# Low parts of the weight tiles made by VectorE instead of GpSimd, in a two-layer diffusion step on one core

## The chip, the core and the metric

The kernel is one program on one core of a Trainium2 chip. TensorE multiplies matrices, VectorE and ScalarE work element by element on SBUF and PSUM, GpSimd on SBUF alone, and SyncE issues most of the DMAs. The engines run apart from each other, each through its own queue in order, and meet at semaphores. In the rows PE is TensorE, PEld its weight loads, DVE VectorE, ACT ScalarE, POOL GpSimd, SP SyncE; a q behind a name (SPq, ACTq) is the engine's queue issuing DMAs. The metric is the device time of one execution in microseconds.

## The reference

Two layers (DEPTH = 2) run over 512 latent tokens and 128 prompt tokens of width 1024. Cut to its core, a layer is:

```python
h = rms_norm(x, g_pre) * (1 + scale) + shift            # scale, shift, gate from silu(cond) @ w_mod
parts = split(h @ w_in)                                 # w_in: 1024 x 10752
y_sg = spatial_gating(sg_u, sg_v, ...)
y_diff = diff_attention(dq, dk, dv, lam)                # 4 heads, two softmax maps per head
y_na = neighbourhood_attention(nq, nk, nv, ...)         # 8 heads, 8 x 16 window and the context keys
y_f = fourier_mix(h)
mixed = sum(sigmoid(merge[b]) * ((y[b] * silu(gate[b])) @ proj[b]) for b in four branches)
x = x + gate * rms_norm(mixed @ w_o, g_post)
```

All of it is in float32. The outputs are the tokens after both layers and the prompt's keys and values.

## The kernel before

TensorE multiplies in the rounded float32 form (fp32r), which keeps fewer bits than float32. So each operand is split into a high part (rounded) and a low part (value minus high part), and a product is three matmuls: high with high, high with low, low with high (`three`, and the loop in the steps F, M and P).

The weights come as 224 tiles ("slots") of 128 x 1024, in the order in which they are used. For slot n: SyncE loads it into `raw`, of which there are two buffers (RAWS = 2), and waits before that for `lo` of slot n-2; ScalarE copies it into `whi`, which rounds it (`high`, five buffers, SPLITS = 5); GpSimd computes `wlo = raw - whi` (`low`). TensorE waits for `lo` of a slot before its first matmul with it.

The order of everything is one list of 1273 steps, `PLAN.seq`. Every engine runs through this list, does its share of each step and waits on semaphores whose counts are worked out from the list. The steps that the prediction speaks of are: HK, HL and TK (the first layer's h, its low part, and the first product with it), VS and VN (sum of squares and norm of sg_v; the power of -1/2 between them is GpSimd's), F (a projection), M and P (a merge gate and a projected branch, each some 7 us of TensorE), S, EX, CB, TP and PV (scores, exponentials, combination of the two softmax maps, transposes, and product with V of one attention unit), NM (normalisation in the neighbourhood attention), DM (one dot product of a deferred modulation tile), FB (back transform of the Fourier branch), T (a wide projection, with the names sgv, dq, dk, dv, wo0 and wo1), Ya, Yb, Xa, Xb and H (from one layer's output to the next layer's h). In the attention stages F, M and P are cut in parts (PART) that fill the gaps between the attention's steps, so that the steps there are short. `FENCE` lets an engine catch up with the others at a change of stage.

`PLAN.issue` says at which step slots are split: slot n at the first step that uses slot n-4, or right after the last use of slot n-5, whichever is later. ScalarE runs `high` at the beginning of that step, GpSimd `low` in its own queue when it comes to the same step.

GpSimd's other work is the powers: one per tile in Xa, VS and Ya, and one for five tiles in NR (`power` and `root`).

Of the kernel before, what the change touches and what calls it, by code (L numbers as in the profile page):

```python
# [167 lines left out]
WIDE = KT  # L168
LEAD = AHEAD
ASIDE = 4  # L170


def parts(steps):
# [216 lines left out]
class Plan:  # L390


    def __init__(self):
# [43 lines left out]
        for n in range(slot):  # L437
            if n < len(lead_in):
                floor = self.at[0, ("HK", lead_in[n])]
            i = max(self.first_of_slot[n - AHEAD] if n >= AHEAD else start,  # L440
                    self.last_of_slot[n - SPLITS] + 1 if n >= SPLITS else start)
            if self.layer[self.first_of_slot[n]] and self.steps[self.first_of_slot[n]] == ("T", "sgv", 3, 0):
                floor = self.at[1, ("T", "sgv", 0, 2)]
            self.issue.setdefault(max(i, floor), []).append(n)
        self.stream, self.entry = [], {}
        waiting = [(sum(first < i for first in self.first_of_slot.values()) + LEAD, ("D", s[1]))
                   for i, s in enumerate(self.steps) if s[0] == "DM"]
# [91 lines left out]
def program(nc, A, O):  # L539
    with ExitStack() as ctx:  # L540
# [184 lines left out]
        def _(pool):  # L725
# [21 lines left out]
            for i, (layer, step) in enumerate(PLAN.seq):  # L747
                count.at(i)
                kind = step[0]
                for s in PLAN.issue.get(i, ()):  # L750
                    low(s)
                if kind == "Xa":
                    j = step[1]
                    pool.wait_ge(sems["epsd"], count.step("epsd"))
                    power(stats[:, XST, 1, j:j + 1], stats[:, XST, 0, j:j + 1])
                elif kind == "VS":
                    j = step[1]
                    pool.wait_ge(sems["xss"], count.step("xss"))
                    root(VST, j, ss[:, 1, j:j + 1], 512)
                elif kind == "Ya":  # L760
                    j = step[1]
                    pool.wait_ge(sems["epsd"], count.step("epsd"))
                    power(stats[:, YST, 1, j:j + 1], stats[:, YST, 0, j:j + 1])
                elif kind == "NR" and step[3] == 1:
                    pool.wait_ge(sems["epsd"], count.step("epsd"))
                    power(rstd[:, 0:TILES], veps[:, 0:TILES])
# [304 lines left out]
        def _(dve):  # L1071
# [20 lines left out]
            if True:  # L1092
# [7 lines left out]
                for i, (layer, step) in enumerate(PLAN.seq):  # L1100
                    count.at(i)
                    b = PLAN.buf.get(i)
                    kind = step[0]
                    hT, act = held(layer)
                    if kind == "FENCE" and i + 1 < len(PLAN.steps):

                        for name, n in count.phase(i):
# [907 lines left out]
```

## Time and profile before

| | us |
|---|---|
| median of 3 runs (1981.74 to 1983.77) | 1981.79 |
| the profiled execution | 1982.85 |
| its span, first to last instruction | 1980.9 |
| TensorE busy in it | 1903.0 |
| VectorE busy | 960.9 |
| ScalarE busy | 678.3 |
| GpSimd busy | 593.8 |

The span is 1.95 us shorter than the execution's own time, which also holds what lies around the instructions. The profiled execution is 1.06 us above the median of the runs. Mean granted clock of TensorE is 0.989 of full speed. Times in the trace are microseconds from the start of the span. "Idle before" an instruction is shown in brackets with what ended it.

### The profile page before, as it was taken

The numbers are of one execution on the slowest core, as the hardware profiler recorded it, in microseconds if no ns is written. First come the engines' busy times: TensorE is split into PE (matmuls) and PEld (weight loads), VectorE is DVE, ScalarE is ACT, GpSimd is POOL, SyncE is SP. The second block draws the span as 40 slices with busy tenths as digits, with TensorE's granted clock in tenths as the row PEclk, the third lists the DMA queues.
The fourth block names the chain that finished last, engine by engine and source line by source line (L and its number), as shares of the span: only waits on it lengthen the run. The fifth ranks groups of instructions, "written<-read, shape, count | busy, mean of one in ns | idle before, by whom it ended". The sixth has DMA issues, their size and how long they took to land.

```text
span 1980.9 us, 31159 instructions
## 1 busy us (share of the span) xinstructions
PE 1903.0 (96%) x12512; PEld 1762.9 (89%) x12512; DVE 960.9 (49%) x1536; ACT 678.3 (34%) x1293; POOL 593.8 (30%) x278
## 2 busy tenths in 40 slices
PE   6799999999999999999999999999999999999997
PEld 3697888989999999999878988988999999999996
DVE  5799788634355462421352144666244546433123
ACT  4322355424433221321352234453334332222221
POOL 2434322222222332233334332222322223323331
PEclk8999999999999999999999999999999999999999
DMA  8444421121111211122332221111212112212231
GB/s 305 145 164 140 164 97 43 54 83 67 65 65 65 94 66 54 65 75 75 128 117 75 91 75 65 49 49 43 96 65 75 54 65 95 75 35 83 75 126 55
DMA packets 50958, 172.16 MB, mean 87 GB/s; under 512 B 6656, under 2 KB 7296, under 8 KB 50816
## 3 DMA queue, kind: packets, MB, share of 16 engines
q1 hardware_dynamic: 41024, 146.60, 21.3%
q10 hardware_dynamic: 9792, 23.58, 3.3%
q8 instruction: 99, 1.62, 0.3%
q14 instruction: 43, 0.35, 0.1%
HBM read 162.82 MB, written 7.34 MB: 86 GB/s over the span
## 4 chain that ended last, share of the span: by engine, by line
PE 80%; DVE 12%; issue 3%; ACT 3%; DMA 1%; POOL 0%; SPq 0%; ACTq 0%; DVEq 0%; POOLq 0%
PE ps L1661 56%; PE ps L1549 4%; PE ps L1551 4%; PE ps L1550 4%; DVE mixed L1089 3%; PE ps L1768 2%; PE ps L1777 1%; PE ps L1787 1%; PE ps L1727 1%; PE ps L1742 1%; DMA stage<-in_w_mod 1%; DVE nparts L1313 1%; ACT Pm L998 1%; DVE Pm L1375 1%; PE ps L1812 1%
## 5 line engine op out<-in xcount | busy, mean ns | idle before, releaser
L733 POOL TENSOR_TENSOR wlo<-raw,whi 128x1024 fp32r<-128x1024 f32 x224 | 563.4, 2515 | 1233.0 <-ACT whi L791 1230.6
L1661 PE MATMUL ps<-bufB,whi 128*128 128x320 f32 x2816 | 539.4, 314 | 7.1 <-DVE vn L1215 3.9
L1661 PE MATMUL ps<-bufA,whi 128*128 128x320 f32 x2816 | 537.3, 313 | 5.3 <-DVE z L1495 1.4
L1661 PEld LDWEIGHTS ps<-bufB,whi 128*128 128x128 f32 x2816 | 441.4, 189 | 16.9 <-issue 12.3
L1661 PEld LDWEIGHTS ps<-bufA,whi 128*128 128x128 f32 x2816 | 439.3, 188 | 15.0 <-issue 10.4
L1661 PE MATMUL ps<-bufB,wlo 128*128 128x320 f32 x1408 | 322.0, 310 | 0.0
L1661 PE MATMUL ps<-bufA,wlo 128*128 128x320 f32 x1408 | 321.4, 309 | 0.0
L791 ACT ACTIVATE whi<-raw 128x1024 fp32r<-128x1024 f32 x224 | 237.5, 1060 | 212.3 <-PE ps L1661 123.6
L1661 PEld LDWEIGHTS ps<-bufB,wlo 128*128 128x128 f32 x1408 | 236.3, 189 | 0.0
L1661 PEld LDWEIGHTS ps<-bufA,wlo 128*128 128x128 f32 x1408 | 235.7, 188 | 0.0
L1495 DVE SCALAR_TENSOR_TENSOR z<-gate_m,ps 128x640 f32<-128x640 f32 x48 | 39.4, 821 | 226.2 <-PE ps L1661 225.6
L1089 DVE CUSTOM_DVE_ANT_0 mixed<-stage,mixed 128x1024 f32<-128x1024 f32 x80 | 135.1, 1689 | 3.2 <-DVE bufB L1097 0.5
L1033 ACT ACTIVATE gate_m<-ps 128x640 f32<-128x640 f32 x64 | 45.2, 706 | 207.1 <-PE ps L1661 196.3
L1549 PE MATMUL ps<-whi,bufA 128*128 128x512 f32 x240 | 96.9, 404 | 13.0 <-DVE bufA L1204 12.1
L1549 PE MATMUL ps<-whi,bufB 128*128 128x512 f32 x240 | 95.4, 397 | 0.6 <-POOL wlo L733 0.6
L1551 PE MATMUL ps<-whi,bufA 128*128 128x512 f32 x240 | 95.0, 396 | 0.0
L1550 PE MATMUL ps<-wlo,bufA 128*128 128x512 f32 x240 | 94.9, 395 | 0.0
L1551 PE MATMUL ps<-whi,bufB 128*128 128x512 f32 x240 | 94.2, 393 | 0.0
L1550 PE MATMUL ps<-wlo,bufB 128*128 128x512 f32 x240 | 94.2, 392 | 0.0
L738 POOL TENSOR_TENSOR stats<-stats,neghalf 128x1 f32<-128x1 f32 (+1 forms) x38 | 28.0, 736 | 144.3 <-DVE stats L1406 75.2
L1549 PEld LDWEIGHTS ps<-whi,bufA 128*128 128x128 f32 x240 | 46.1, 192 | 23.8 <-POOL wlo L733 9.4
L988 ACT ACTIVATE Pm<-ps,nmax 128x384 f32<-128x384 f32 (+1 forms) x80 | 43.1, 539 | 65.1 <-DVE nmax L1329 64.9
(230 smaller groups left out, 2043.1 us busy)
## 6 DMA issues: line engine op xcount, KB each, us to landing
raw<-in_wstream SPq DMA_DIRECT2D x224, 512.0 KB, 3.2
stage<-in_wstream SPq DMA_DIRECT2D x32, 512.0 KB, 4.2
stage<-in_w_mod SPq DMA_DIRECT2D x16, 512.0 KB, 15.2
out_y_sample<-X ACTq DMA_DIRECT2D x8, 512.0 KB, 2.7
Pm<-in_rpb ACTq DMA_DIRECT2D x12, 256.0 KB, 2.9
X<-in_x_sample SPq DMA_DIRECT2D x4, 512.0 KB, 10.9
xres<-in_x_sample ACTq DMA_DIRECT2D x4, 512.0 KB, 5.1
xres<-out_y_sample ACTq DMA_DIRECT2D x4, 512.0 KB, 5.2
```

Source lines behind the costliest of these rows:

```text
L733: pool.tensor_tensor(wlo[:, s % SPLITS, :], raw[:, s % RAWS, :], whi[:, s % SPLITS, :].bitcast(F32), ALU.subtract).then_inc(sems["lo"], 1)
L738: pool.tensor_tensor(out, src, neghalf[:, 0:out.shape[-1]], ALU.pow).then_inc(sems["powd"], 1)
L791: act_e.activation(whi[:, s % SPLITS, :], raw[:, s % RAWS, :], ACT.Copy).then_inc(sems["hi"], 1)
L988: act_e.activation(dst, src, ACT.Exp, bias=nmax[:, slot:slot + 1], accum_out=esum[:, slot:slot + 1]).then_inc(sems["expd"], 1)
L1033: act_e.activation(halves(gate_m[:, m % 2, :]), dsplit(b), ACT.Tanh, scale=0.5).then_inc(sems[f"free{b}"], 1)
L1089: yield dve.tensor_tensor_reduce(dots_out, src, rows[:, c, :], 0.5, 0.0, ALU.mult, ALU.add, mods[:, l, 2 * m + c:2 * m + c + 1])
L1495: dve.scalar_tensor_tensor(halves(dst), halves(gate_m[:, m % 2, :]), 1.0, dsplit(b), ALU.add, ALU.mult).then_inc(sems[f"free{b}"], 1)
L1549: pe.matmul(out, stat_hi, mov_hi, start=first, stop=False)
L1550: pe.matmul(out, stat_hi, mov_lo, start=False, stop=False)
L1551: return pe.matmul(out, stat_lo, mov_hi, start=False, stop=last)
L1661: ins = pe.matmul(ps[:, 2 * b + n, 0:HALF], wt[:, cols], src[:, part, base + k, n * HALF:(n + 1) * HALF], start=k == 0 and wt is hi and pa ...
L1768: ins = pe.transpose(ps[:, bank, at:at + P], src[:, c * P:(c + 1) * P], ident[:])
```

## The change

GpSimd keeps the low parts of the first five slots and all powers. The low parts of the other 219 slots are made by VectorE, each with one instruction of the same shape. In the list of steps their place is two steps behind ScalarE's high part, or the step before the slot's first use where that comes earlier. ScalarE's and TensorE's instructions stay as they were, and so do SyncE's and what each of them waits for; `lo` is now counted up by VectorE.

```diff
@@ -168,6 +168,8 @@
 ASIDE = 4
+OPENING = 5
+BEHIND = 2
@@ -442,6 +444,12 @@
             self.issue.setdefault(max(i, floor), []).append(n)
+        self.split = {}
+        for i, made in self.issue.items():
+            for n in made:
+                at = i if n < OPENING else min(i + BEHIND, self.first_of_slot[n] - 1)
+                assert at < self.first_of_slot[n]
+                self.split.setdefault(max(at, i), []).append(n)
@@ -747,8 +755,9 @@
-                for s in PLAN.issue.get(i, ()):
-                    low(s)
+                for s in PLAN.split.get(i, ()):
+                    if s < OPENING:
+                        low(s)
@@ -1102,6 +1111,14 @@
+                    for n in PLAN.split.get(i, ()):
+                        if n >= OPENING:
+                            if n == OPENING:
+                                dve.wait_ge(sems["lo"], OPENING)
+                            dve.wait_ge(sems["hi"], n + 1)
+                            dve.tensor_tensor(wlo[:, n % SPLITS, :], raw[:, n % RAWS, :],
+                                              whi[:, n % SPLITS, :].bitcast(F32), ALU.subtract).then_inc(sems["lo"], 1)
+                            dve.wait_ge(sems["lo"], n + 1)
```

The line numbers of the changed kernel are 8 to 17 higher than those of the kernel before. Three places in the queues show what moves.

GpSimd's queue from the end of layer 0 (the powers of Ya and Xa) to VS of layer 1, before. `wlo` is the low part, L743 and L738 are the two instructions of VS:

```order
L733 TENSOR_TENSOR wlo<-raw,whi 128x1024 x2
L738 TENSOR_TENSOR stats<-stats,neghalf 128x1 x3
L733 TENSOR_TENSOR wlo<-raw,whi 128x1024 x5
L743 TENSOR_SCALAR stats<-ss 128x1
L738 TENSOR_TENSOR stats<-stats,neghalf 128x1
L743 TENSOR_SCALAR stats<-ss 128x1
L738 TENSOR_TENSOR stats<-stats,neghalf 128x1
```

The same stretch in the changed kernel, from the four powers of layer 0's NR on:

```order
L746 TENSOR_TENSOR stats<-stats,neghalf 128x5 x4
L746 TENSOR_TENSOR stats<-stats,neghalf 128x1 x10
L751 TENSOR_SCALAR stats<-ss 128x1
L746 TENSOR_TENSOR stats<-stats,neghalf 128x1
L751 TENSOR_SCALAR stats<-ss 128x1
L746 TENSOR_TENSOR stats<-stats,neghalf 128x1
```

The subtractions between the powers are gone, and so are the five in front of VS.

VectorE's queue in the differential attention of layer 0, before. L1355 is PV of one unit, L1337 to L1345 are CB of unit 5, L1313 begins the maximum over the next unit's scores:

```order
L1355 TENSOR_SCALAR yb<-ps,rsum 128x128
L1337 TENSOR_TENSOR esum<-esum,ectx 128x2
L1339 RECIPROCAL rsum<-esum 128x2
L1342 SCALAR_TENSOR_TENSOR comb_c<-rsum,lam,esum 128x1
L1345 SCALAR_TENSOR_TENSOR Pm<-Pm,comb_c 128x640
L1313 TENSOR_REDUCE nparts<-ps 128x2
```

After; L1372 is PV, L1354 the first instruction of CB:

```order
L1372 TENSOR_SCALAR yb<-ps,rsum 128x128
L1119 TENSOR_TENSOR wlo<-raw,whi 128x1024
L1354 TENSOR_TENSOR esum<-esum,ectx 128x2
L1356 RECIPROCAL rsum<-esum 128x2
L1359 SCALAR_TENSOR_TENSOR comb_c<-rsum,lam,esum 128x1
L1362 SCALAR_TENSOR_TENSOR Pm<-Pm,comb_c 128x640
L1330 TENSOR_REDUCE nparts<-ps 128x2
```

A subtraction stands ahead of the combination of the unit, and waits for ScalarE's high part of its slot.

VectorE's queue from layer 0 to layer 1, before. L1242 is the scaling of the first half of the output rows, L1112 and L1115 are the modulation of layer 1, L1222 is the scaling of the second half, tile 0, and L1519 the new residual:

```order
L1242 TENSOR_TENSOR X<-ps,grow 128x512 x5
L1112 TENSOR_TENSOR modv<-mods,bmod 128x32
L1115 SCALAR_TENSOR_TENSOR amul<-modv,gpre 128x16
L1222 TENSOR_TENSOR X<-ps,grow 128x512
L1179 TENSOR_TENSOR ss<-ssy 128x1
L1181 TENSOR_SCALAR stats<-ss 128x1
L1519 SCALAR_TENSOR_TENSOR X<-X,stats,xres 128x1024
```

After:

```order
L1259 TENSOR_TENSOR X<-ps,grow 128x512 x5
L1119 TENSOR_TENSOR wlo<-raw,whi 128x1024
L1129 TENSOR_TENSOR modv<-mods,bmod 128x32
L1132 SCALAR_TENSOR_TENSOR amul<-modv,gpre 128x16
L1119 TENSOR_TENSOR wlo<-raw,whi 128x1024 x2
L1239 TENSOR_TENSOR X<-ps,grow 128x512
L1196 TENSOR_TENSOR ss<-ssy 128x1
L1198 TENSOR_SCALAR stats<-ss 128x1
L1536 SCALAR_TENSOR_TENSOR X<-X,stats,xres 128x1024
```

Five subtractions have come in, two of them between the modulation and the first tile of the second half.

## Rows read from the trace of the kernel before

**Rows 1.** The page: busy time of the engines over the span.

```profile
PE 1903.0 (96%) x12512; PEld 1762.9 (89%) x12512; DVE 960.9 (49%) x1536; ACT 678.3 (34%) x1293; POOL 593.8 (30%) x278
```

**Rows 2.** The page: the DMA issues of raw (KB each, median us to landing).

```profile
raw<-in_wstream SPq DMA_DIRECT2D x224, 512.0 KB, 3.2
```

**Rows 3.** Who waited for whom, TensorE: releaser, us in total, times, longest.

```profile
PE ps L1549 <- DVE bufA L1204: 12.1, 4, 6.5
...
PE ps L1742 <- ACT Pm L998: 5.7, 6, 1.4
PE ps L1661 <- DVE vn L1215: 4.9, 2, 3.9
PE ps L1747 <- DVE yb L1355: 4.4, 6, 1.5
...
PE ps L1577 <- DVE mixed L1209: 3.4, 1, 3.4
...
PE ps L1661 <- DVE z L1495: 2.7, 2, 1.4
...
PE ps L1768 <- DVE Pm L1375: 2.4, 5, 0.6
...
PE ps L1687 <- DVE qr L1265: 1.4, 1, 1.4
```

**Rows 4.** VectorE in order of time, 58 to 72: start, duration, instruction.

```profile
59.55 1.23 DVE L1089 CUSTOM_DVE_ANT_0 mixed<-stage,mixed 128x1024 f32<-128x1024 f32 x1
...
65.13 3.24 DVE L1089 CUSTOM_DVE_ANT_0 mixed<-stage,mixed 128x1024 f32<-128x1024 f32 x1
...
68.68 2.19 DVE L1154 SCALAR_TENSOR_TENSOR amul<-mods,bmod,gpre 128x2 f32<-128x2 f32 x1
```

**Rows 5.** GpSimd in order of time, 58 to 83.

```profile
61.61 5.69 POOL L733 TENSOR_TENSOR wlo<-raw,whi 128x1024 fp32r<-128x1024 f32 x2 [9.62 <-ACT whi L791]
```

**Rows 6.** The window after the first gap: us, busy per engine (instructions), TensorE clock, DMA.

```profile
72.00:77.00 5.00, 5.00 (x12) 3.95 (x13) 2.82 (x15) 2.23 (x4) 0.54 (x1) 0.50 0.99 363
```

**Rows 7.** VectorE groups with shapes kept apart: busy, mean ns.

```profile
L1199 DVE TENSOR_TENSOR bufB<-hz,bufB 128x1024 fp32r<-128x1024 f32 x3 | 3.7, 1225 | 1.3 <-ACT bufB L843 1.3
```

**Rows 8.** ScalarE, GpSimd, VectorE in order of time before TensorE's wait at 1051.04.

```profile
1044.60 1.06 ACT L791 ACTIVATE whi<-raw 128x1024 fp32r<-128x1024 f32 x1 [4.39 <-DMA raw<-in_wstream]
...
1045.81 2.38 POOL L733 TENSOR_TENSOR wlo<-raw,whi 128x1024 fp32r<-128x1024 f32 x1 [1.97 <-ACT whi L791]
...
1049.23 0.75 DVE L1215 SCALAR_TENSOR_TENSOR vn<-ps,stats,gvb 128x512 f32<-128x512 f32 x1 [13.27 <-POOL stats L738]
```

**Rows 9.** The windows after the gap at 1047 to 1051.

```profile
1051.00:1057.00 6.00, 5.96 (x23) 5.99 (x24) 2.25 (x3) 0.00 (x0) 3.86 (x5) 0.51 0.13 37
1057.00:1063.00 6.00, 6.00 (x43) 6.00 (x43) 0.82 (x1) 1.76 (x2) 0.03 (x1) 1.00 0.13 53
```

**Rows 10.** Layer 0's differential attention in order of time, and its window 285 to 303.

```profile
284.95 1.06 ACT L791 ACTIVATE whi<-raw 128x1024 fp32r<-128x1024 f32 x1
...
285.02 0.16 DVE L1337 TENSOR_TENSOR esum<-esum,ectx 128x2 f32<-128x2 f32 x1 [1.05 <-ACT Pm L1004]
...
285.67 0.89 DVE L1345 SCALAR_TENSOR_TENSOR Pm<-Pm,comb_c 128x640 f32<-128x640 f32 x1
...
288.97 0.71 PE L1768 MATMUL ps<-ident,Pm 128*128 128x128 f32 x5
...
285.00:303.00 18.00, 17.79 (x134) 16.65 (x132) 16.57 (x35) 9.88 (x26) 4.28 (x3) 1.00 0.17 60
```

**Rows 11.** TensorE and VectorE where the neighbourhood attention of layer 0 begins.

```profile
450.58 0.17 DVE L1371 RECIPROCAL rsum<-esum 128x2 f32<-128x2 f32 x1 [0.76 <-ACT Pm L988]
...
451.45 0.44 PE L1768 MATMUL ps<-ident,Pm 128*128 128x128 f32 x2 [0.43 <-DVE Pm L1375]
```

**Rows 12.** VectorE from layer 0 to layer 1, in order of time.

```profile
987.12 0.69 DVE L1222 TENSOR_TENSOR X<-ps,grow 128x512 f32<-128x512 f32 x1 [4.29 <-ACT junk L802]
...
1014.20 2.39 DVE L1179 TENSOR_TENSOR ss<-ssy 128x1 f32<-128x1 f32 x1
```

## The prediction

> **What bounds the kernel now.** I read the page first. TensorE is busy for 1903.0 of 1980.9 us [rows 1], so 78 us is all that any change outside TensorE's own work could give back, and the reader is to ask for every cost below whether TensorE waits for it. Next the list of waits of TensorE [rows 3]. Of the waits, 6.5 us in one piece hang on the last pieces of h in the opening, 3.9 on the norm of sg_v, and 3.4 on the normalised x of layer 1. The rest are many small ones, mostly in the attention stages, where ScalarE or VectorE is a little late. GpSimd is named in none of them, though its low parts make up nearly all of its 593.8 busy us [rows 1]. So the question is what GpSimd's subtractions do to others, and what the same work does inside VectorE's queue.
>
> VectorE in order of time answers the first part. The dot product of L1089 takes 1.23 us at 59.55 and 3.24 at 65.13 [rows 4]; an operation on two columns takes 2.19 us at 68.68. GpSimd's subtractions run from 61.61 to 67.30 [rows 5], and the next one covers the last case. So a VectorE instruction that begins just after a subtraction of GpSimd stands still until that is over, at some 2 us a time.
>
> Amounts below that no single row gives come about so. I wrote out the instructions of VectorE, ScalarE, GpSimd and SyncE, kept TensorE's times as they are, gave prolonged VectorE instructions the shortest length of their shape, put the low parts in their new places, and let each instruction begin when its queue and what it waits for allow it. What TensorE waits for then comes earlier or later by so much. Done with the kernel as it is, this gives nine of ten starts back within 0.4 us.
>
> **Removed: GpSimd's 219 subtractions.** First the opening. The chain dot product, modulation, h, TensorE's TK 6 holds both prolonged instructions, so it is ready 2.0 + 2.0 = 4.0 us earlier. It does not give 4 us. In the changed queue two low parts follow the two pieces of h, then raw 7 can be loaded, and ScalarE's high part 7 stands ahead of VS. I get: pieces of h done at 71.3, low part 5 at 72.6, raw 7 landed 3.2 us later [rows 2] at 75.8, its high part done at about 77.0, tile 0 and 1 of VN done at 80.4, where TensorE needs them for the first F at 82.5 now. That is a gain of 2.0. Against it stands the clock. It was at 0.50 in 72 to 77 after the 6.5 us wait [rows 6]. Now the wait moves behind TK 7, and the half clock may fall on the first F, at up to 3.4 us. Bounds +2.0 and -1.4; I take a gain of 1, since half of the old loss disappears in any case.
>
> Second, the small waits. Those of S, PV, TP, QT, P and M that are ended by VectorE, or by ScalarE after VectorE, are the rows L1742, L1747, L1661 behind z, L1768 behind L1375 and L1687 of [rows 3], 5.7 + 4.4 + 2.7 + 2.4 + 1.4 = 16.6 us. I went through them in order of time and counted only those with a prolonged VectorE instruction in front, each at the smaller of the wait and the 2 us: 15 waits of 0.25 to 1.44, 9.6 us together. Bounds 16.6 and 0 (if the prolonging has another cause).
>
> Third, layer 1's VN, the largest item. Before 1051.04 ScalarE stood 4.39 us for raw data, which waited for GpSimd's two low parts in a row; then GpSimd made another low part from 1045.81 to 1048.19 before it came to the powers of VS; VectorE's first VN began at 1049.23 [rows 8]. VectorE makes those low parts in 1.23 each, raw comes 1.2 us earlier, and the powers no longer queue behind a 2.38 us subtraction. VN begins 3.0 us earlier, and TensorE's wait shrinks from 3.9 to 0.8. After the long wait the clock was 0.51 for 6 us, and 23 matmuls took what full clock does in 6.0 x 23 / 43 = 3.2 [rows 9]. Without it another 2.8 comes back. Together 5.9 (bounds 3.1 and 5.9; I take 5.9, as waits of 0.8 stand in many places at full clock).
>
> **Added: 219 subtractions on VectorE.** One is 1225 ns, by the same shape from L1199 [rows 7]: 268 us more on VectorE, 49% busy now. Most lies under TensorE: in the branch stages (M, P and F at 7 us each) VectorE has over 4 us free per step, and a slot's low part is done more than 10 us before use. There the later low part delays raw n+2 by up to two steps, and ScalarE stands up to 6.4 us at a high part; its Tanh of the step is then 0.5 us late against a reserve of one whole step. Hidden; it would cost 7 us per step if the reserve weren't there.
>
> In the short steps of attention it isn't hidden. At 285.02 VectorE begins CB, while ScalarE is at the high part, 284.95 to 286.01 [rows 10]. The subtraction has come in ahead of CB: VectorE waits 1.1 for the high part, subtracts 1.23, and CB is 2.5 us late. CB's last instruction ends at 286.56, and TP on TensorE begins at 288.97 [rows 10], of which 0.2 is the way between them: 2.2 in hand. In layer 0 dot products fill VectorE, 16.57 of 18 us busy from 285 to 303 [rows 10], so it can't catch up: TensorE loses 2.3 there, and 0.6 in two later units (bounds 0 and 4.3). In layer 1, without dot products, 0.4. Where neighbourhood attention begins, the low part stands ahead of NM; VectorE at 450.58 would wait until 451.6 and subtract: 2.5 late, with TensorE already waiting [rows 11]: 2.3 in layer 0, 1.4 in layer 1 where 1.0 was in hand. A gap of this size could halve the clock for some microseconds; I put 1.0 for both.
>
> From layer 0 to 1 two low parts stand ahead of tile 0's scaling at 987.12 [rows 12], one of them waiting for a high part whose raw has waited for a low part too: 2.1 late, TensorE likewise. But the 2.39 us at 1014.20 [rows 12] becomes 0.2, and TensorE's 3.4 us wait behind it takes up most of the slip: 1.1 remain, and the shorter wait (2.3) may keep the clock up, worth 0 to 2.8; I take 1.4. Smaller ones: M, m = 5 of branch 2 0.8 in both layers, F fgate 0.5, dq 0.3, the last wo1 0.2, layer 0's last differential unit 0.3.
>
> **Sum.** Gains 1.0 + 9.6 + 5.9 + 1.4 = 17.9. Losses 2.3 + 0.6 + 0.4 + 2.3 + 1.4 + 1.0 + 1.1 + 0.8 + 0.5 + 0.3 + 0.2 + 0.3 = 11.2. Net 6.7 off the profiled execution's 1982.85 is 1976.2. That execution was 1.06 above the median of the runs, by which the sum is 1975.1. As costs of a queue are easier to overlook than gains, I take 1976.5.
>
> **Rivals.** (a) The two halves cancel: chance 0.32. Half clock still falls behind 1051 or in the opening, and the new gap at 451 brings it as well. For: each of the three long waits of now has it. Then 2.8 + 1.4 + 1.4 go: 1976.5 + 5.6 = 1982.
>
> (b) Slower, chance 0.14: VectorE's queue in attention becomes the bound. About 15 slots fall in each layer's differential attention, and 16 more in its neighbourhood attention; each wait for a high part plus subtraction is 2.5 us against some 2.2 in hand, by [rows 10]. I count 0.3 to 0.4 over at only a few. If the true reserve is 0.5 us smaller, the 30 differential ones cost 15 us more: 1991. The point from which it decides is a reserve of 2.2 us; against it, VectorE gets back 2 us at each prolonged instruction in the same stretch. The Trainium skill, Perfetto Trace Analysis, section Optimizing Scalar/DVE Operations, speaks for this rival: work is to be moved off VectorE, even to GpSimd, where VectorE is saturated; it adds that a move between these two may not help because they share a port. No run here yet shows which half of that holds; by its first half the time would be the 1991, by its second the 1982 of (a).
>
> (c) The prolonging isn't GpSimd's doing (it could be DMA writes in the same moments), so the change does not do what it removes: chance 0.05. Then the 9.6 and the 1.0 go, VN's gain stays: 1987. Against it: at 59.55 with DMAs running, 1.23 as elsewhere.
>
> My own case has 0.49: faster by 5 us, its range 1970 to 1980. All together: low 1969 (bounds of the small waits and the clock both for it), high 1988 (rival c inside, half of b). About 0.2%, 4 us, is what a measurement of this kernel can tell from no change; 0.47 of my case's 0.49 is counted below that, the rest of it and (a) within, (b) and (c) above: faster 0.47, same 0.34, slower 0.19.
>
> **What would show it.** L1215's wait behind VN in layer 1 falls from 3.9 to below 1, with full clock at 1051. L1089 is 1.23 us in every instance after the opening. GpSimd is busy about 45 us. New waits of TensorE appear at TP in the first neighbourhood unit and near 294 and 302 us. ScalarE's wait for raw grows to several hundred us without a wait of TensorE behind it. I am wrong if TensorE waits for CB in most units, if the half clock has moved rather than gone, or if TensorE waits for `wlo`.

## The result, and the profile after

The changed kernel takes 1984.99 us in the median (20 runs, 1979.44 to 1989.00); the kernel before takes 1981.93 (20 runs, 1980.06 to 1983.77). The ratio is 1.0014, with a 95% interval of 1.0007 to 1.0020: 3 us slower, less than the 4 us that the prediction took as what can be told from no change, yet with this many runs the interval leaves no change out. The forecast was 5 us faster. The spread is a result too: 9.6 us from the quickest to the slowest run, against 3.7 before. Of the runs of the kernel before that stand beside later experiments, two, of 2108 and 3860 us, are left out.

The profiled execution of the change is one of its quickest, 1981.16 us with a span of 1979.3, so its trace alone can't show the loss. Its page, as in [rows 1]:

```profile
PE 1903.1 (96%) x12512; PEld 1763.1 (89%) x12512; DVE 1088.9 (55%) x1755; ACT 678.2 (34%) x1293; POOL 48.6 (2%) x59
...
L800 ACT ACTIVATE whi<-raw 128x1024 fp32r<-128x1024 f32 x224 | 237.5, 1060 | 325.6 <-DMA raw<-in_wstream 232.8
L1119 DVE TENSOR_TENSOR wlo<-raw,whi 128x1024 fp32r<-128x1024 f32 x219 | 268.3, 1225 | 127.2 <-ACT whi L800 113.7
...
L1098 DVE CUSTOM_DVE_ANT_0 mixed<-stage,mixed 128x1024 f32<-128x1024 f32 x80 | 106.4, 1330 | 3.2 <-DVE bufB L1106 0.5
```

The work moved as intended: GpSimd has 48.6 us left, VectorE's 219 low parts take 1225 ns each, and the dot product (L1098, formerly L1089) has a mean of 1330 ns, down from 1689; what is left above 1225 are four of them in the opening, beside GpSimd's first five low parts. [rows 4] shows one at 1.23 us alone and one at 3.24 beside GpSimd. TensorE's waits, which answer to [rows 3] (releaser, us in total, times, longest):

```profile
PE ps L1678 <- DVE vn L1232: 9.6, 2, 8.4
PE ps L1566 <- DVE bufA L1221: 8.0, 4, 2.4
PE ps L1764 <- DVE yb L1372: 5.3, 3, 2.1
...
PE ps L1785 <- DVE Pm L1392: 3.5, 2, 2.5
...
PE ps L1759 <- ACT Pm L1007: 3.3, 5, 1.1
...
PE ps L1566 <- DVE wlo L1119: 0.4, 2, 0.2
```

The wait for the pieces of h fell from 6.5 to 2.4 at its longest, as worked out, and a wait of 8.4 us for `vn` stands in its place. TensorE hardly waits for `wlo` itself. Two rows of the kernel before belong beside these, since the prediction read that list without them:

```profile
PE ps L1768 <- DVE Pm L1345: 3.0, 3, 1.4
...
PE ps L1549 <- POOL wlo L733: 0.6, 1, 0.6
```

GpSimd was named once, with 0.6 us. And TensorE already waited three times for the last instruction of CB (L1345), so the 2.2 us in hand that the prediction read at one unit weren't there at all of them.

**Layer 1's VN** came out nearly as forecast. GpSimd, VectorE in order of time, and the window behind (its columns as in [rows 6]):

```profile
1046.47 0.50 POOL L751 TENSOR_SCALAR stats<-ss 128x1 f32<-128x1 f32 x1 [21.49 <-ACT junk L811]
...
1047.74 0.75 DVE L1232 SCALAR_TENSOR_TENSOR vn<-ps,stats,gvb 128x512 f32<-128x512 f32 x1 [0.82 <-POOL stats L746]
...
1050.00:1057.00 7.00, 7.00 (x50) 7.00 (x49) 1.81 (x3) 0.37 (x2) 1.07 (x3) 1.00 0.01 2
```

No subtraction stands ahead of the powers, the wait fell from 3.9 to 1.2 (9.6 less 8.4; 0.8 was forecast), and the seven us behind it hold 50 matmuls at full clock, where [rows 9] had 23 in six.

**The opening** did not. VectorE, ScalarE and TensorE in order of time, and the window behind the wait:

```profile
71.46 2.48 DVE L1119 TENSOR_TENSOR wlo<-raw,whi 128x1024 fp32r<-128x1024 f32 x2
...
81.78 0.75 DVE L1232 SCALAR_TENSOR_TENSOR vn<-ps,stats,gvb 128x512 f32<-128x512 f32 x1 [0.81 <-POOL stats L746]
...
78.58 1.06 ACT L800 ACTIVATE whi<-raw 128x1024 fp32r<-128x1024 f32 x1 [3.34 <-DMA raw<-in_wstream]
79.67 0.60 ACT L811 ACTIVATE junk<-ps 128x512 f32<-128x512 f32 x1
...
83.59 1.40 PE L1678 MATMUL ps<-bufA,whi 128*128 128x320 f32 x4 [8.42 <-DVE vn L1232]
...
83.00:90.00 7.00, 6.41 (x32) 6.44 (x33) 2.70 (x4) 1.29 (x3) 1.95 (x5) 0.69 0.49 191
```

Low part 5 is done at 72.7 (71.46 + 1.23), within 0.1 of the forecast. But raw 7, issued then, landed at 78.5, 5.8 us later. The issues from 70 to 84 us (the last number is the median to landing):

```profile
raw<-in_wstream SPq DMA_DIRECT2D x3, 512.0 KB, 5.8
...
wsT<-in_sg_wT ACTq DMA_DIRECT2D x1, 512.0 KB, 3.6
```

ScalarE stood 3.34 us at the high part, the sums of squares (L811) began at 79.67, and the first F at 83.59 in place of 82.46, with half clock behind it.

**Differential attention of layer 0**, the place of [rows 10]. VectorE, TensorE and two windows:

```profile
286.17 1.23 DVE L1119 TENSOR_TENSOR wlo<-raw,whi 128x1024 fp32r<-128x1024 f32 x1 [2.14 <-ACT whi L800]
287.43 0.16 DVE L1354 TENSOR_TENSOR esum<-esum,ectx 128x2 f32<-128x2 f32 x1
...
295.86 0.80 PE L1764 MATMUL ps<-cK,QT 64*128 64x128 f32 x4 [2.13 <-DVE yb L1372]
...
285.00:295.00 10.00, 8.73 (x67) 7.93 (x63) 8.41 (x15) 5.25 (x13) 0.00 (x0) 1.00 0.30 106
295.00:303.00 8.00, 7.14 (x30) 6.94 (x31) 7.55 (x16) 1.44 (x2) 0.00 (x0) 0.57 0.01 2
```

The low part came in ahead of CB (its first instruction is L1354), which began at 287.43 in place of 285.02: 2.4 late, where 2.5 was forecast, and TensorE lost 1.9 more than before (2.13, against 0.21 at the same matmul), where 2.3 was forecast. Then the clock was 0.57 over eight us, some 6.9 us at half, which costs half of that, 3.4 us, and which no term of the forecast held.

### The profile page after: what moved, and what is told of

It is laid out like the page before. It is cut to its first block, busy times and chain, and to the rows that moved or that the text cites. A ratio compares the mean times of both kernels' runs of the same rounds, so it can differ in the third digit from the quotient of the medians.

```text
span 1979.3 us, 31155 instructions
## 1 busy us (share of the span) xinstructions
PE 1903.1 (96%) x12512; PEld 1763.1 (89%) x12512; DVE 1088.9 (55%) x1755; ACT 678.2 (34%) x1293; POOL 48.6 (2%) x59
## 3 DMA queue, kind: packets, MB, share of 16 engines
q1 hardware_dynamic: 41024, 146.60, 21.8%
## 4 chain that ended last, share of the span: by engine, by line
PE 44%; DVE 3%; ACT 2%; issue 1%; DMA 0%; POOL 0%; ACTq 0%; DVEq 0%; POOLq 0%
PE ps L1678 30%; PE ps L1566 2%; PE ps L1568 2%; PE ps L1567 2%; PE ps L1785 1%; PE ps L1794 1%; PE ps L1804 1%; DVE wlo L1119 1%; PE ps L1759 1%; PE ps L1744 1%; ACT Pm L1007 0%; ACT whi L800 0%; DVE X L1536 0%; PE ps L1829 0%; PE ps L1691 0%
## 5 line engine op out<-in xcount | busy, mean ns | idle before, releaser
L1119 DVE TENSOR_TENSOR wlo<-raw,whi 128x1024 fp32r<-128x1024 f32 x219 | 268.3, 1225 | 127.2 <-ACT whi L800 113.7
L1512 DVE SCALAR_TENSOR_TENSOR z<-gate_m,ps 128x640 f32<-128x640 f32 x48 | 39.4, 821 | 178.8 <-PE ps L1678 178.2
L1098 DVE CUSTOM_DVE_ANT_0 mixed<-stage,mixed 128x1024 f32<-128x1024 f32 x80 | 106.4, 1330 | 3.2 <-DVE bufB L1106 0.5
```

The source lines that it names most:

```text
L1098: yield dve.tensor_tensor_reduce(dots_out, src, rows[:, c, :], 0.5, 0.0, ALU.mult, ALU.add, mods[:, l, 2 * m + c:2 * m + c + 1])
L1119: dve.tensor_tensor(wlo[:, n % SPLITS, :], raw[:, n % RAWS, :], whi[:, n % SPLITS, :].bitcast(F32), ALU.subtract).then_inc(sems["lo"], 1)
L1512: dve.scalar_tensor_tensor(halves(dst), halves(gate_m[:, m % 2, :]), 1.0, dsplit(b), ALU.add, ALU.mult).then_inc(sems[f"free{b}"], 1)
```

## The experiments

GpSimd makes low part n where `on_gpsimd(n)` holds, right behind its high part; VectorE makes it elsewhere, by the changed kernel's rule. This edit underlies all kernels but `after_again`, `vs_first` and `behind0`; `open12` has it as `OPENING = 12`.

```diff
-                at = i if n < OPENING else min(i + BEHIND, self.first_of_slot[n] - 1)
+                at = i if on_gpsimd(n) else min(i + BEHIND, self.first_of_slot[n] - 1)
...
```

A second edit, called "behind CB" below, adds under it:

```diff
+                if not on_gpsimd(n) and self.steps[max(at, i)][0] in ("CB", "NM"):
+                    at = max(at, i) + 1
```

All results together. The clock is the mean of the granted clock over the runs. "Lost" is (1 - clock) x span, "rest" is the mean span less that. Both are worked out, and a clock printed to 0.001 leaves them about 0.6 us uncertain; the kernel before moves by up to 1.0 in them from one group of runs to the next, so differences between groups are no better than that.

"Lost" is more than what half clock took, since it also counts half clock over an idle TensorE. Every profile ends with 5 to 8 us at half clock in which no matmul runs. The last stretch of the kernel before (columns as in [rows 6]):

```profile
1975.30:1980.90 5.60, 0.00 (x0) 0.00 (x0) 0.00 (x0) 0.00 (x0) 0.00 (x0) 0.50 0.23 95
```

Of the 21.7 us lost in that profile 6.9 lie over an idle TensorE, and in the two profiles of the change 8.2 and 7.6. So where a reading rests on this split, a second one stands beside it, from single profiles: the sum of TensorE's waits, and the span less that sum. It is 67.4 and 1913.5 us for the kernel before.

| kernel | runs | median us | ratio to before (95%) | clock | lost | rest |
|---|---|---|---|---|---|---|
| before (beside after_again and the three under it) | 29 | 1981.98 | | 0.9897 | 20.4 | 1959.7 |
| the change | 20 | 1984.99 | 1.0014 (1.0007 to 1.0020) | 0.9860 | 27.7 | 1955.4 |
| after_again | 11 | 1985.43 | 1.0015 (1.0006 to 1.0024) | 0.9861 | 27.6 | 1955.8 |
| open12 | 9 | 1977.17 | 0.9979 (0.9969 to 0.9989) | 0.9892 | 21.3 | 1955.0 |
| vs_first | 11 | 1979.34 | 0.9987 (0.9978 to 0.9996) | 0.9873 | 25.2 | 1952.6 |
| attn_gp | 9 | 1987.73 | 1.0028 (1.0018 to 1.0038) | 0.9884 | 22.9 | 1963.0 |
| before (beside the next four) | 23 | 1982.17 | | 0.9892 | 21.4 | 1958.7 |
| behind_cb | 5 | 1969.25 | 0.9932 (0.9919 to 0.9944) | 0.9918 | 16.1 | 1950.8 |
| trans_gp | 8 | 1977.49 | 0.9975 (0.9965 to 0.9985) | 0.9885 | 22.7 | 1952.7 |
| open_only | 11 | 1985.54 | 1.0019 (1.0010 to 1.0028) | 0.9890 | 21.8 | 1962.3 |
| attn_dve | 11 | 1981.55 | 1.0000 (0.9991 to 1.0009) | 0.9878 | 24.1 | 1956.2 |
| before (beside the next four) | 14 | 1982.07 | | 0.9896 | 20.6 | 1959.3 |
| cb_only | 5 | 1973.05 | 0.9954 (0.9941 to 0.9966) | 0.9904 | 18.9 | 1952.1 |
| cb_trans | 5 | 1967.77 | 0.9927 (0.9914 to 0.9941) | 0.9910 | 17.7 | 1947.9 |
| best | 4 | 1965.24 | 0.9915 (0.9902 to 0.9929) | 0.9915 | 16.7 | 1946.7 |
| attn_gp12 | 11 | 1985.54 | 1.0014 (1.0005 to 1.0023) | 0.9891 | 21.6 | 1961.3 |
| before (beside the next two) | 11 | 1981.93 | | 0.9896 | 20.5 | 1959.5 |
| cb_half | 7 | 1975.80 | 0.9968 (0.9957 to 0.9979) | 0.9906 | 18.6 | 1955.1 |
| behind0 | 5 | 1990.26 | 1.0043 (1.0030 to 1.0055) | 0.9860 | 27.8 | 1960.5 |

**after_again**: the changed kernel, no edit.

> The changed kernel once more, nothing edited, for another profiled execution. Its 20 runs lay between 1979.4 and 1989.0 us with a mean granted clock of 0.989 to 0.984, while the kernel before lay between 1980.1 and 1983.8; the execution profiled first was one of its quickest (1981.16). Theory A (the clock): the waits of TensorE add up to the same within 2 us, and what differs from execution to execution is how many pieces of half clock there are; at 1984 to 1988 us there are one to three pieces of 3.4 or 6.8 us more than in the first profile, each behind a wait of 1 to 3 us that was there at full clock in the first profile. Theory B (VectorE's queue): the slower executions have longer waits of TensorE for VectorE, with the clock as before. Time about 1985.

Theory A holds in the main. Its profiled execution has a span of 1983.6; TensorE's waits add up to 64.2 us, against 65.7 in the first profile, and half clock before the end covers 47.8 us, against 37.5. Not each piece is behind a wait that was there at full clock before, as theory A had it: most of the difference lies in longer or additional pieces in the opening and in layer 1's H. One does, in layer 1's attention. In the first profile, and then in this one, TensorE at one place of layer 1, with a window behind it:

```profile
1223.95 0.49 PE L1764 MATMUL ps<-cK,QT 64*128 64x128 f32 x4 [1.65 <-DVE yb L1372]
...
1225.00:1229.00 4.00, 4.00 (x31) 3.99 (x30) 3.40 (x5) 1.22 (x2) 0.00 (x0) 1.00 0.01 4
```

```profile
1226.78 0.49 PE L1764 MATMUL ps<-cK,QT 64*128 64x128 f32 x4 [1.65 <-DVE yb L1372]
...
1228.00:1232.00 4.00, 4.00 (x19) 4.00 (x18) 3.23 (x5) 0.86 (x1) 0.00 (x0) 0.57 0.01 4
```

The wait is 1.65 us both times, behind the same instruction. Once 31 matmuls follow in four us, once 19. In the table the change has a smaller rest than before (4.3 us) and loses 7.3 more: +3.0, the measured slowdown. By the second reading the waits of the two profiles are 1.7 and 3.2 us shorter than before, and the spans less the waits 0.1 and 5.9 longer. The execution near the median (1985.43) is the second, and it agrees with the table; the first, one of the quickest, has none of the loss.

**open12**: `OPENING = 5` becomes 12.

> GpSimd keeps the low parts of slots 0 to 11 in place of 0 to 4, so the opening is the one of the kernel before; VectorE makes the rest. In the changed kernel the first F of the opening began 1.1 us later than before, and half clock right behind it made that 2.6. Theory A: low part 5 on VectorE is what keeps raw 7 and so the high part that stands ahead of VS; here the first F is back at 82.5 with half clock at 70 to 77 as before, and the time is 2.6 below that of the changed kernel, 1982.4. Rival: the opening doesn't matter, since a wait given back there returns at full clock further on; then the same as the changed kernel within 1.

It gained 8.3 over after_again, three times what was expected, and 6.3 of it in "lost". That the opening matters is shown; the amount isn't the opening's alone, as cb_only and behind_cb show (3.8 between them).

**vs_first**: the high part of slot 7 behind the sums of squares.

```diff
-            self.issue.setdefault(max(i, floor), []).append(n)
+            self.issue.setdefault(self.at[0, ("VN", 4)] if n == 7 else max(i, floor), []).append(n)
```

> The changed kernel with one step moved: ScalarE makes the high part of slot 7 behind the sums of squares of sg_v (at VN of tile 4) and not ahead of them. In the changed kernel ScalarE stood at that high part until raw 7 landed at 78.5 us, while TensorE had ended TK 7 at 75.2. Theory A: the first VS begins at 75.3, the first two vn are done at 79.1, and the first F begins at 79.2 in place of 83.6: 4.4 us gained, and 2.9 more if half clock doesn't fall behind the wait of 4 that remains; 1980.6 or 1977.7. Rival: GpSimd's powers or the load of gvb are late by themselves, and the first F doesn't begin before 82.

6.1 below after_again, between the two figures of theory A. TensorE's wait for `vn` in the opening fell from 8.9 us in after_again's profile to 4.3. So what was late there was first of all a high part standing at a transfer ahead of VS. Of what is left, the rival's `gvb` has a share: VectorE stood 1.17 us for it before the first VN.

```profile
78.98 3.89 DVE L1232 SCALAR_TENSOR_TENSOR vn<-ps,stats,gvb 128x512 f32<-128x512 f32 x5 [1.17 <-DMA gvb<-in_sg_norm_g]
```

**attn_gp**: `on_gpsimd(n)` is `n < 5 or 28 <= n < 72 or 140 <= n < 184`.

> GpSimd makes the low parts in the two attention stages of both layers (slots 28 to 71 and 140 to 183) and of the first five slots; VectorE makes all others. Theory A: the gaps at 294 and 453 us that VectorE's queue made are gone, and with them the half clock behind them; the median falls by 3 to 5 us to 1980 to 1982, and the runs lie within 4 us of one another as those of the kernel before. Theory B (the prolonging is what costs in attention, by the 9.6 us of small waits that the forecast hoped for): VectorE's instructions are prolonged again and the time rises by up to 9 us over the changed kernel. Rival: neither, since both are small, and the time stays at 1985 with the same spread.

2.3 above after_again, theory B's direction: the rest grew by 7.2 while 4.7 came back from "lost". Where attention starts, GpSimd, VectorE, TensorE and the window behind:

```profile
240.55 2.40 POOL L746 TENSOR_TENSOR wlo<-raw,whi 128x1024 fp32r<-128x1024 f32 x1 [153.94 <-ACT whi L807]
...
240.77 2.20 DVE L1343 TENSOR_TENSOR nmax<-nparts 128x2 f32<-128x2 f32 x1
...
244.56 1.50 PE L1766 MATMUL ps<-KTt,QT 64*128 64x256 f32 x8 [1.97 <-ACT Pm L1014]
...
245.00:249.00 4.00, 4.00 (x23) 3.60 (x20) 3.73 (x9) 0.80 (x4) 0.00 (x0) 0.57 0.69 232
```

An operation on two columns, 0.16 us at 248.82 in the same trace, took 2.20, begun 0.22 behind GpSimd's subtraction and ended with it; ScalarE's exp and TensorE followed late, and half clock came behind. The Trainium skill, GPSIMD Engine Reference, section Specifications, says that GpSimd's way to SBUF is shared with VectorE and that VectorE's instructions with two SBUF inputs contend with it; the trace agrees, since this one has two. All of VectorE's instructions in the kernel before that began inside a subtraction are counted in the last section.

**behind_cb**: the rule "behind CB" above, with `n < 12`. It moves 24 low parts by one step: 10 that stood ahead of CB, 14 ahead of NM.

> On top of open12 (GpSimd keeps slots 0 to 11; 1977.2 us): where a low part stood on VectorE ahead of CB or of NM, it stands one step later, behind it. Theory A (each such low part makes VectorE wait for ScalarE's high part and CB come 2.5 us late): the gaps of 2.1 near 294 and 2.0 near 453 us go, with the pieces of half clock that sometimes follow them; 3 to 6 us less than open12, 1971 to 1974. Rival: the low part now stands ahead of the maximum that ScalarE's exp waits for, the gaps come back in front of S, and the time is that of open12 or up to 4 us more.

7.9 less than open12, more than theory A's 3 to 6, about half in the rest and half in "lost". ScalarE's wait for raw is as long as in the change, and is harmless:

```profile
ACT whi L809 <- DMA raw<-in_wstream: 229.0, 51, 11.6
```

**trans_gp**: `n < 12 or 108 <= n < 112`.

> On top of open12: GpSimd makes slots 108 to 111 as well, those of the change from layer 0 to layer 1. Theory A: the 1.9 to 2.1 us that every version with these on VectorE lost against the kernel before between 948 and 997 us are gone, and about half of it comes back at the wait for the normalised x further on; 1 to 2 us less than open12, 1975 to 1976. Rival: GpSimd's subtractions prolong VectorE's there as in the kernel before, and nothing is gained: 1977 to 1978.

The median is open12's and in the rival's range. The rest is 2.3 lower and "lost" 1.4 higher, so theory A's gain may be there and be lost again to half clock; by this run alone that isn't shown.

**open_only**: `not 5 <= n < 12`.

> The kernel before with one part of the change alone: VectorE makes slots 5 to 11, of the opening, and GpSimd all others. Theory A (the opening is where the change loses): open12 against the changed kernel showed 4.1 us of direct loss up to 294 us and about as much again further on; so 4 to 8 us above the kernel before, 1986 to 1990. Rival: the 8 us between the changed kernel and open12 were mostly chance of where half clock fell; then within 2 us of the kernel before, 1982 to 1984.

3.4 above the kernel before, between the rival's 2 and theory A's 4 to 8. The opening costs this by itself.

**attn_dve**: `not (28 <= n < 72 or 140 <= n < 184)`.

> The kernel before with another part of the change alone: VectorE makes the low parts of the attention stages (slots 28 to 71 and 140 to 183), GpSimd all others. The complement of attn_gp, which was 2.3 us above the changed kernel. Theory A (in attention the move helps, since VectorE's small instructions are no longer prolonged, by more than its queue costs): 2 to 5 us below the kernel before, 1977 to 1980. Theory B (VectorE's queue becomes the bound in attention): 2 to 9 us above it.

Neither range was met: 1.0000. The rest is 2.5 lower, "lost" 2.7 higher. With low parts ahead of CB and NM, VectorE's queue costs what the end of the prolonging gives.

**cb_only**: "behind CB" with `n < 5`, so the change with those 24 low parts moved and nothing else.

> The changed kernel with one edit: a low part that stood on VectorE ahead of CB or NM stands one step later. The opening is the changed kernel's own, with its late first F. Theory A (two places lose independently: the opening 8, the low parts ahead of CB and NM 8): 1985.4 less 8, 1977.5. Rival (the 8 us that behind_cb gained over open12 need the opening's shift as well, since where the half clock falls decides): 1980 to 1984.

12.4 below after_again, more than either theory: one step's difference in the order of 24 instructions is worth about four times the slowdown.

**cb_trans**: "behind CB" with `n < 12 or 108 <= n < 112`.

> behind_cb (1969.3 us) with slots 108 to 111 on GpSimd. On top of open12 this gave 2.1 us back at 997 and 1.1 more by 1056, but the median stayed at 1977.5, with more half clock in the attention of layer 1. Theory A: with the gaps of that attention gone there is nothing left for half clock to fall on, and the 2 to 3 us stay: 1966.5. Rival: they are lost further on again, 1969.

In between: 1.5 less than behind_cb, with overlapping intervals. The rest is 2.9 lower, "lost" 1.6 higher.

**best**: "behind CB", `n < 5 or 108 <= n < 112`, and vs_first's edit.

> All that helped, together: low parts behind CB and NM; slots 0 to 4 and 108 to 111 on GpSimd; and ScalarE's high part 7 behind the sums of squares in place of slots 5 to 11 on GpSimd. In the profiles the first F of vs_first began 2.9 us before that of open12. Theory A: 2.9 less than cb_trans should be, 1963.6. Rival: the wait of 4 us that vs_first leaves in front of the first F brings half clock in most executions, and the time is that of cb_trans or above, 1966 to 1968.

1965.2 in four runs, 2.5 below cb_trans, between theory A and its rival, with overlapping intervals. The wait ahead of the first F remains:

```profile
78.41 0.95 PE L1687 MATMUL ps<-bufA,whi 128*128 128x320 f32 x4 [3.71 <-DVE vn L1241]
```

It is the quickest version run, 0.85% below the kernel before (0.71 to 0.98).

**attn_gp12**: `n < 12 or 28 <= n < 72 or 140 <= n < 184`. It differs from behind_cb in the low parts of those 88 slots: their engine, and with it their place, which is right behind the high part in place of two or three steps later. The 24 that behind_cb moved are among them.

> behind_cb with the attention stages (slots 28 to 71 and 140 to 183) back on GpSimd, VectorE's low parts elsewhere. What is taken away against behind_cb is only that VectorE's instructions there aren't prolonged, and VectorE's queue there is shorter. Theory A (the prolonging costs about the 9.6 us of small waits that the forecast took, most of them in attention): 1969.3 plus 8 to 11 with the clock's part, 1977 to 1980. Rival (the prolonging costs TensorE little, and behind_cb gained because it undid a self-made delay): 1969 to 1973.

16.3 above behind_cb, where theory A had 8 to 11: 10.5 in the rest and 5.5 in "lost". The two profiles say the same: waits of 67.5 us against 57.4, and 1913.1 against 1908.5 for the span less the waits. TensorE's waits, behind ScalarE's exp, here and then in behind_cb:

```profile
PE ps L1766 <- ACT Pm L1014: 9.7, 8, 2.0
```

```profile
PE ps L1768 <- ACT Pm L1016: 3.0, 4, 1.1
```

**cb_half**: the rule for CB alone.

> The changed kernel with only the ten low parts that stood ahead of CB moved one step later; the fourteen ahead of NM stay. In the forecast the ten had 3.3 us (2.3 + 0.6 + 0.4) and the fourteen 4.7 (2.3 + 1.4 + 1.0 for the clock); cb_only moved all and gained 12.4. Theory A (both cost, in the forecast's proportion): 5.1 of the 12.4, so 1980.3. Rival (the NM ones cost nearly all, since TensorE waits already there): 1984. Second rival (the CB ones do, ten times over): 1975.

The second rival, nearly: 9.6 below after_again. Its rest is that of after_again within 0.7, and 9.0 of the gain is in "lost". Its profile against after_again's has it less one-sided: 2.7 us less in waits and 6.9 less in the rest of the span. The wait at 294, where the change has 2.13, is half as long, and full clock follows:

```profile
294.93 0.49 PE L1773 MATMUL ps<-cK,QT 64*128 64x128 f32 x4 [1.10 <-DVE yb L1381]
```

The fourteen low parts ahead of NM are the step from here to cb_only: 3.0 in the rest, nothing in "lost".

**behind0**: `BEHIND = 0`.

> The changed kernel with the low parts made at the step of their high part in place of two steps later. ScalarE's wait for raw (232.8 us in the changed kernel) should fall below 60, and VectorE's wait for the high part should grow. Theory A (late raw data is harmless; what costs is VectorE's wait in front of an instruction that TensorE needs): no gain from raw, and VectorE's waits for ScalarE come in more units: 1984 to 1990. Rival (the late raw data costs, since ScalarE's high part holds up what stands behind it): 1975 to 1981.

Theory A, just above its range. TensorE's waits for VectorE, and VectorE's for ScalarE:

```profile
PE ps L1764 <- DVE yb L1372: 18.3, 10, 2.7
```

```profile
DVE wlo L1119 <- ACT whi L800: 329.0, 116, 7.1
```

ScalarE's wait for raw fell to 20.6 us, VectorE's wait for the high part grew from 113.7 to 329.0, and the kernel is 4.8 slower than after_again. Behind the opening, raw data that comes late costs nothing that shows; VectorE standing at a low part does. In the opening it does cost, since ScalarE stands at raw 7 ahead of the sums of squares (vs_first).

## Why the forecast was wrong

Split as in the table, the forecast had 3.5 us of gain outside the clock (1.0 + 9.6 + 3.1, less 10.2) and 3.2 in it (2.8 + 1.4, less 1.0). Measured were 4.3 of gain outside and 7.3 of loss in it (1.7 to 3.2 less waiting, and 0.1 to 5.9 more in the rest of the span, by the two profiles). **The first sum came out near its total, partly because errors in its terms cancel; the step that failed is "A gap of this size could halve the clock for some microseconds; I put 1.0 for both"**, for among the new waits of the attention stages it priced the clock only at 451 and its like in layer 1. It left it out at the gap near 294, where 3.4 us went in the first profile, and at every smaller one, as at 1684, where half clock follows a wait of 1.8 us in both profiles of the change.

How far the change stands behind the kernel before (minus: ahead), from the starts of the same matmuls in both traces, for its two profiles:

| us in the kernel before | 95 | 284 | 320 | 440 | 460 | 940 | 1019 | 1056 | 1680 | 1950 |
|---|---|---|---|---|---|---|---|---|---|---|
| first profile | 2.8 | 0.1 | 2.5 | 0.0 | 2.0 | 1.0 | 2.4 | -4.1 | -4.0 | -1.5 |
| after_again | 5.7 | 3.0 | 4.0 | 1.5 | 3.4 | 2.4 | 3.7 | -1.3 | 0.4 | 2.8 |

Point by point:

- **Opening, taken as a gain of 1.0: wrong in sign.** Up to the end of low part 5 the working holds within 0.1. It failed at "raw 7 landed 3.2 us later [rows 2]": a median over the kernel was used for a moment at which `wsT`, `bsb`, `gvb` and the next entries of the stream were in flight. It took 5.8. In the kernel before raw 7 landed in 3.4 us, issued ahead of `wsT` and the others; in the change these came first, at 70.5 in place of 73.0, since h was done earlier. That the company is the cause is read from this order; no run separates it. The opening costs 3.4 (open_only), 3.8 (behind_cb against cb_only), or 8.3 where the rest of the change stands behind it (open12).
- **Small waits, 9.6: the mechanism right, the size too high.** In the attention stages alone low parts on GpSimd in place of VectorE cost 10.5 in the rest, plus 5.5 in "lost" (attn_gp12 against behind_cb), and with GpSimd's subtractions the long versions of VectorE's instructions are gone. So rival (c) is out. But attn_gp12 also waits 4.0 us longer behind ScalarE's exp than the kernel before, so the 10.5 isn't what that kernel had to give. The five rows of the forecast's 16.6 us [rows 3] add up to 15.6 in the first profile of the change and to 11.1 in behind_cb's (3.0 + 4.6 + 3.5; two are gone): 1.0 and 5.5 came back. The change got less of it because its own low parts stood in the way.
- **VN of layer 1, 5.9: right** by its wait, 2.7 shorter where 3.1 was forecast, and its full clock. By the same matmuls, the change gained 5.3 us on the kernel before between 1025 and 1056, and attn_dve, which leaves these low parts on GpSimd, gained 0.2 there.
- **Low parts ahead of CB, 3.3: the time of VectorE right, the price wrong.** Undoing them gave 9.6, most of it in the clock (cb_half: 9.0 by the table, 6.9 by the profiles). They lengthen waits in places that already wait a little, and a wait of 1.65 or 2.13 us is enough for half clock in some executions.
- **Low parts ahead of NM, 3.7 and 1.0 for the clock: right in the first**, 3.0, and the clock's part was nothing. The wait at 453 was 2.48, or 2.05 more than in [rows 11], for 2.3 forecast:

```profile
453.47 0.44 PE L1785 MATMUL ps<-ident,Pm 128*128 128x128 f32 x2 [2.48 <-DVE Pm L1392]
```

- **Layer 0 to 1, 1.1: about right.** The lateness at tile 0 is there: by the same matmuls the change fell 2.3 us further behind from 940 to 1010 in both profiles, and had made up 0.9 and 1.0 of it at 1019, so 1.4 and 1.3 remain. That 2.3 (trans_gp) and 2.9 (cb_trans) came out of the rest when these low parts stayed on GpSimd isn't the same quantity, since those versions keep the gain at 1014 too. (The queue that is printed for this stretch shows three subtractions, not five.)
- **Clock at H of tile 3, 1.4: unsettled.** It was at half for 3.4 us in place of 6.8 in the first profile, and for 6.8 in the second.
- **Late raw data hidden: right, but for raw 7 in the opening.** behind_cb has 229.0 us of it and is 13 us quicker than the kernel before; behind0 has 20.6 and is the slowest of all.
- **The signs.** Of those named for being wrong one came: the half clock has moved rather than gone. TensorE doesn't wait for CB in most units, and waits 0.4 us for `wlo`.
- **Rival (a)** described the outcome best: half clock moves rather than goes, 1982. It was held to the opening, 1051 and 451: right in the opening, wrong at 1051, and at 451 half clock stands in one profile of the later kernels (vs_first) and in neither of the change. Its sum takes off 1.4 twice, and only one of these is a term of the forecast. **Rival (b)**, that VectorE's queue in attention becomes the bound, is refuted in its main form: with attention back on GpSimd the kernel is 2.3 slower (attn_gp), and moving attention alone changes nothing (attn_dve). What it said of the reserve at CB was nevertheless where most of the loss sat. The Trainium skill, Perfetto Trace Analysis, section Optimizing Scalar/DVE Operations, has two halves; neither gives the result. VectorE wasn't saturated (55% busy), and in attention, with the low parts behind CB and NM, moving work from GpSimd to VectorE helped by 10.5 us in the rest, where the second half says that a move between these two might not help.

**What stays open.** attn_gp12 has the opening of the kernel before and VN's gain of layer 1, yet its rest is 2.0 above that kernel's; its waits behind ScalarE's exp are 9.7, against 5.7 in [rows 3]. That GpSimd, idle till then, begins each subtraction at a worse moment would explain it, and was not tried; 15 of the small operations ahead of exp (`nmax<-nparts`) are prolonged there, against 12 in the kernel before. Why half clock falls behind a given wait in one execution and not in another wasn't found, only that it does. The figures of "best" and cb_trans rest on four and five runs.

## What to carry to other kernels

When work goes from one in-order queue to another, look not at the busy share but at what stands behind each new instruction, and put it behind the instruction that TensorE is waiting for and not ahead: one step's difference for 24 of 219 instructions was 12 us, four times the whole effect of the move. Price every wait of TensorE above a microsecond twice, once as the wait and once as a chance of half clock behind it, and judge a change by several executions and their mean clock, since one profiled execution can miss the loss entirely. Ask of a helper engine not only how busy it is, but which of VectorE's instructions begin inside its own. Take a transfer's landing time from what is in flight at that moment, and ask what the change itself moves there.

## What the runs showed of the hardware

- The same wait of 1.65 us in the same kernel was followed by full clock once (31 matmuls in 4 us) and by a granted clock of 0.57 over 4 us in another execution (19 matmuls). The Trainium skill, TensorE: Matmul & The Clock Gate, Part 1, says that how many matmuls run at the low clock at a kernel's start varies from run to run of one kernel; the runs show such a difference in the middle of a kernel too. The quickest run of the change had a mean clock of 0.988 at a span of 1977.6 us and the slowest 0.984 at 1987.2, by which about 8 of the 9.6 us between them are half clock (1 or 2 us either way, by the rounding of the clock).
- Over 15 kernels, (1 - clock) x span lay between 16.1 and 27.8 us of some 1980, with 5 to 8 us of it over an idle TensorE in the profiles. It changed by 9.0 us through an edit that left the rest within 0.7 (cb_half).
- A VectorE instruction of 0.16 us took 2.20 beside a GpSimd subtraction of 2.40; without GpSimd's subtractions in attention TensorE's waits behind ScalarE's exp fell from 9.7 to 3.0 us.
- Not every VectorE instruction stands still, as the prediction has it. In the trace of the kernel before 209 of them began inside a subtraction of GpSimd, more than 0.4 us before its end. 85 were prolonged, by 144 us in all: every one with two tensors from SBUF (the 19 dot products, the 12 `nmax<-nparts`), and also 22 with one tensor from SBUF to SBUF and a scale (the 18 of L1375 and 4 of L1512). None of the 124 others was: the copies, scalings and sums with an operand in PSUM, the 27 maxima (12 of them from SBUF), the 18 reciprocals, the 17 reads of the dot products' sums and 2 small operations on a constant (L1443).
- A load of 512 KB landed in 5.8 us where three loads of ScalarE's queue and others of SyncE's ran beside it, in 3.4 where it was issued ahead of those three, and in 3.2 in the median.
